# Four gate pairs of the second block computed as seven products, with fixed weight tiles and the memory's preparation moved

## The reference, cut to what matters

```python
branch_a = o_a @ w_branch_a[l]          # 512 -> 1024
branch_b = y_b @ w_branch_b[l]          # 512 -> 1024
merged = jax.nn.sigmoid(g_a) * branch_a + jax.nn.sigmoid(g_b) * branch_b
x = x + merged @ w_mix_out[l]
x = x + memory_cross_attention(rms_norm(x, norm_mem_q[l]), rms_norm(mem, norm_mem_kv[l]), ...)
```

## Time and profile before

| | us |
|---|---|
| median of 3 runs | 1548.76 (1548.67 to 1548.92) |
| profiled execution, its own time | 1548.38 |
| span of the trace | 1546.6 |
| PE busy | 1536.8 (99%) |
| DVE busy | 1055.0 (68%) |
| ACT busy | 754.5 (49%) |
| POOL busy | 69.1 (4%) |

### The profile page before, as it was taken

How to read it: one execution, slowest core, us unless ns; L and a number is a source line. 1 busy time by engine, 2 the same in 40 slices (tenths; PEclk the granted TensorE clock), 3 DMA queues, 4 the chain that set the end, 5 groups by cost and what they waited for, 6 DMA issues and landing times.

```text
span 1546.6 us, 22323 instructions
## 1 busy us (share of the span) xinstructions
PE 1536.8 (99%) x8348; PEld 1330.0 (86%) x8348; DVE 1055.0 (68%) x1755; ACT 754.5 (49%) x1307; POOL 69.1 (4%) x60
## 2 busy tenths in 40 slices
PE   9999999999999999999999999999999999999998
PEld 7888888888899899888888888888888899989987
DVE  6776887768789575447777545555555899948735
ACT  5446677744457445444544334344444445524514
POOL 0000000020000000210000010020002000000002
PEclk9999999999999999999999999999999999999999
DMA  5333222332323233324351242334123333322322
GB/s 195 122 109 97 88 78 93 103 129 90 127 84 110 96 96 108 97 82 131 118 141 62 71 137 87 118 118 156 55 82 109 110 103 110 124 96 82 110 89 75
DMA packets 56235, 161.88 MB, mean 105 GB/s; under 512 B 7232, under 2 KB 8640, under 8 KB 56000
## 3 DMA queue, kind: packets, MB, share of 16 engines
q1 hardware_dynamic: 55504, 159.41, 31.7%
q0 software_dynamic: 320, 0.52, 0.2%
q10 hardware_dynamic: 304, 0.52, 0.1%
HBM read 148.89 MB, written 2.10 MB: 98 GB/s over the span
## 4 chain that ended last, share of the span: by engine, by line
PE 96%; DVE 2%; ACT 1%; issue 1%; DMA 1%; SPq 0%; DVEq 0%; ACTq 0%
PE G L1490 66%; PE TP L1490 10%; PE SC L1490 9%; PE O L1490 5%; PE M L1490 5%; PE TP L1946 1%; PE TP L1892 0%; DMA T<-QK 0%; DVE WL L2623 0%; DMA GN<-in_gains 0%; PE TP L1995 0%; ACT L2030 0%; SPq L1465 0%; ACT WH L2033 0%; DVE T L2917 0%
## 5 line engine op out<-in xcount | busy, mean ns | idle before, releaser
L1490 PE MATMUL G<-XGh,WH 128*128 128x512 f32 x920 | 362.2, 394 | 0.0
L2623 DVE TENSOR_TENSOR WL<-RAW,WH 128x1024 fp32r<-128x1024 f32 (+2 forms) x269 | 282.7, 1055 | 116.5 <-ACT WH L2033 116.2
L1490 PE MATMUL G<-XGh,WL 128*128 128x512 f32 x920 | 358.4, 390 | 0.0
L1490 PE MATMUL G<-XGl,WH 128*128 128x512 f32 x920 | 358.3, 389 | 0.0
L2033 ACT ACTIVATE WH<-RAW 128x1024 fp32r<-128x1024 f32 (+2 forms) x275 | 240.0, 881 | 93.3 <-PE G L1490 60.8
L1490 PEld LDWEIGHTS G<-XGh,WL 128*128 128x128 f32 x920 | 172.7, 188 | 36.5
L1490 PEld LDWEIGHTS G<-XGh,WH 128*128 128x128 f32 x920 | 172.8, 188 | 36.1
L1490 PEld LDWEIGHTS G<-XGl,WH 128*128 128x128 f32 x920 | 172.9, 188 | 34.3 <-DVE XGl L2623 0.2
L1490 PE MATMUL G<-MGh,WH 128*128 128x512 f32 x372 | 145.0, 390 | 0.0
L1490 PE MATMUL G<-MGl,WH 128*128 128x512 f32 x372 | 144.8, 389 | 0.0
L1490 PE MATMUL G<-MGh,WL 128*128 128x512 f32 x372 | 144.7, 389 | 0.0
(11 more groups left out here) (443 smaller groups left out, 3268.8 us busy)
## 6 DMA issues: line engine op xcount, KB each, us to landing
RAW<-in_dn SPq DMA_DIRECT2D x30, 512.0 KB, 3.3
RAW<-in_fg SPq DMA_DIRECT2D x22, 512.0 KB, 4.2
RAW<-in_up SPq DMA_DIRECT2D x20, 512.0 KB, 3.4
RAW<-in_g SPq DMA_DIRECT2D x16, 512.0 KB, 3.4
RAW<-in_f SPq DMA_DIRECT2D x14, 512.0 KB, 3.7
X<-in_x SPq DMA_DIRECT2D x16, 256.0 KB, 4.3
RAW<-in_q SPq DMA_DIRECT2D x8, 512.0 KB, 3.3
RAW<-in_k SPq DMA_DIRECT2D x8, 512.0 KB, 3.4
```

The costliest lines, as they stand in the source:

```text
L1490: return e.matmul(dst, st, mv, start=start, stop=stop, skip_group_check=True)
L2623: return e.tensor_tensor(dst, src, hi.bitcast(F32), ALU.subtract)
```

## The change

- Gate pairs n = 4 to 7 are made by seven products (`seven_gates`; pairs `GATED` + n). Their units `sa n`, `sb n` are replaced by seven half-tile units each; `bb n` and `ba n` stay.
- `prepare_gates` makes the input's sums for them: per `kt`, `h` adds XGh and XGl back to fp32 for two tiles, then `s13`, `s2`, `s4`, `s_hi`, `s_lo`, in 13 ticks from ba 0's on. It writes `GATE_SUMS` (parts of QK, Vh, Vl).
- Half tile j of every such pair has slot j (0 to 6); from n = 4 on `bb n` has slot 7 and `ba n` slot 8. The rotation does not advance for them.
- The branch weights from bb 3 on land in `T` tiles of their own (6, then 0 for bb and 1 for ba from n = 4), not in `RAW`. SP waits for the last `s_lo` before bb 4's load.
- The closing part has sigmoids on ACT (`c11`, and `sigmoid` for the other parts); the gates land in one pair of tiles (RB, MSK) for all n from 3 on, so `c22`, `c11` and `c21` wait for `merge_b` of the pair before.
- `mem_load` is moved to behind the seven products of pair 7, its squares to the first three ticks of the mx units, the norm to tick 4, the splits to ticks 7 to 14; the low parts (`mem_lo`) are steps of their own, one tick after each high part.

```diff
+GATED, GATE_FIRST = MID + 20, 4
...
     for n in range(2, 8):
-        u += [("sa", n, 1024), ("sb", n, 1024), ("bb", n, 512), ("ba", n, 512)]
+        if n < GATE_FIRST:
+            u += [("sa", n, 1024), ("sb", n, 1024)]
+        else:
+            u += sevens(GATED - MID + n, GATED - MID + n + 1)
+        u += [("bb", n, 512), ("ba", n, 512)]
...
-            if name == "su":
+            if name == "su" and i[0] >= GATED - MID:
+                keys = (i[1],)
+            elif name in ("bb", "ba") and i >= GATE_FIRST:
+                keys = (7 if name == "bb" else 8,)
+            elif name == "su":
...
+    def prepare_gates(self, start):
+
+        for kt in range(4):
+            for n, kinds in enumerate((("h",), ("s13", "s2"), ("s4", "s_hi"), ("s_lo",))):
+                for kind in kinds:
+                    self.later(start + 3 * kt + n, kind, 2, kt)
+
+    def seven_gates(self, i):
+
+        f = GATED + i
+        for j in range(7):
+            self.tick()
+            if j == 0:
+                for n, kind in ((3, "one_out"), (3, "w_less"), (3, "v_less"), (4, "c22"), (5, "c11"), (6, "c12"), (6, "c21")):
+                    self.later(n, kind, f)
+                self.later(6, "sigmoid", f, 1)
+                self.later(7, "sigmoid", f, 0)
+            self.put("seventh", f, j, self.take("su", (f - MID, j)))
...
+        self.prepare_gates(0)
         for n in range(2):
             branch(n, 0)
             self.put("merge_b", n)
-        self.put("mem_load")
-        for k in range(8):
-            self.later(4 + k, "sq", "mem", k)
-            self.later(20 + k, "mem_split", k)
-        self.later(17, "norm", "mem")
         for n in range(2, 8):
-            gates(n)
+            if n < GATE_FIRST:
+                gates(n)
+            else:
+                self.seven_gates(n)
+            if n == 7:
+                self.put("mem_load")
             branch(n, 1)
             branch(n, 0)
             self.put("merge_b", n)
...
     def memory(self):
+        for k in range(8):
+            self.later(k // 3, "sq", "mem", k)
+            self.later(7 + k, "mem_split", k)
+            self.later(8 + k, "mem_lo", k)
+        self.later(4, "norm", "mem")
...
+                    if (name, i) == ("bb", 3):
+                        e.wait_ge(tb_done, TB["turn_b", 3, 2])
+                    elif name in ("bb", "ba") and i == GATE_FIRST:
+                        e.wait_ge(prep_dve, PREP_DVE["s_lo", 2, 3])
```

More of the change, by code:

```diff
@@ L251, in __init__ @@
         self.fetches, self.pairs = self.tail_loads(), [f for f in range(22) if ("st", f, 0) in self.item_of]
+        self.gated = [GATED + n for n in range(GATE_FIRST, 8)]
         self.middle = [MID + p for p in range(MID_FIRST, MID_FIRST + MID_PAIRS)]
@@ L1369, in _ @@
                         e.wait_ge(prep_dve, PREP_DVE["s_lo", 0, 3])
+                    elif name == "sums" and f == GATED + GATE_FIRST:
+                        e.wait_ge(tb_done, TB["turn_b", 3, 2])
+                    elif name == "sums" and f == GATED + GATE_FIRST + 1:
+                        e.wait_ge(mb_lo, MB["merge_b", 2])
                     if behind:
@@ L1618, in _, with left_of_gates @@
             left_of[6] = lambda kt: (Vh[:, 4 + kt, HALF_S:S], Vl[:, 4 + kt, HALF_S:S])
+            def left_of_gates(j, kt):
+                if j in (0, 1, 3, 5):
+                    s = (0, 1, 3, 5).index(j)
+                    h, l = GATE_SUMS[2 * (s // 2):2 * (s // 2) + 2]
+                    return h[:, s % 2, kt, :], l[:, s % 2, kt, :]
+                k, half = kt if j == 2 else 4 + kt, slice(HALF_S, S) if j == 6 else slice(0, HALF_S)
+                return XGh[:, k, half], XGl[:, k, half]
             for step in steps:
@@ L1677, in _ @@
                     mid = f >= MID
-                    first, second = (f == pair for pair in first_pairs[0 if mid else 1])
+                    gated = f >= GATED
+                    first, second = (f == pair for pair in first_pairs[2 if gated else 0 if mid else 1])
                     wh, wl = w_tile(q) if mid else item_tile(q)
@@ L1681, in _ @@
                     bank = bank[:, 0:HALF_S]
-                    if j == 0:
+                    if gated and (j == 0 and (first or second)):
+                        e.wait_ge(ob_lo, PVB["pv_b", 3])
+                    elif gated and first and j in (1, 3):
+                        e.wait_ge(wtb_lo, 2 * 16)
+                    elif gated and (j == 2 and (first or second)):
+                        e.wait_ge(sb_win, 12)
+                    elif j == 0:
                         if first and mid:
@@ L1720, in _ @@
                         at = slice(kt * P, (kt + 1) * P)
-                        hi, lo = left_of[j](kt)
-                        if first and j in (0, 2):
+                        hi, lo = left_of_gates(j, kt) if gated else left_of[j](kt)
+                        if gated and first and j == 0:
+                            e.wait_ge(prep_dve, PREP_DVE["s_lo", 2, kt])
+                        elif first and j in (0, 2) and not gated:
                             e.wait_ge(prep_dve, PREP_DVE["s_lo" if j == 0 else "a_lo", 0 if mid else 1, kt])
@@ L2114, in _ @@
                         e.wait_ge(d_mem, 16)
+                        if k == 0:
+                            e.wait_ge(w_lo, unit("su", (last_gated - MID, 6)))
                     else:
@@ L2406, in _ @@
                     e.wait_ge(unit_done, gemm_done(step))
-                    e.activation(sgb[n % 2][w], G[:, turn_of[step] % 2, :], ACT.Sigmoid).then_inc(g_moved, 1)
+                    e.activation(sgb[n][w], G[:, turn_of[step] % 2, :], ACT.Sigmoid).then_inc(g_moved, 1)
                 elif kind == "merge_b":
@@ L2526, in _ @@
                     e.wait_ge(*seven_done(f, 4))
[L2527 to L2528 removed]
+                    e.activation(made_in(f)[0][:, 0:HALF_S], SC[:, TURN7[f] % 2, 0:HALF_S],
+                                 ACT.Sigmoid if f >= GATED else ACT.Relu if f >= MID else ACT.Silu).then_inc(seven_act, 1)
+                elif kind == "sigmoid":
+                    f, w = arg
+                    table(ACT.Sigmoid)
+                    e.wait_ge(seven_dve, SEVEN_DVE["c12" if w else "c21", f])
+                    part = made_in(f)[1] if w else made_in(f)[0][:, HALF_S:S]
+                    e.activation(part, part, ACT.Sigmoid).then_inc(seven_act, 1)
                 elif kind == "silu":
@@ L3202, in _ @@
                     b, n = b_tiles(f), TURN7[f]
-                    first = f in (first_pairs[0][0], first_pairs[1][0])
-                    section = 0 if f >= MID else 1
+                    first = f in [pair[0] for pair in first_pairs]
+                    section = 2 if f >= GATED else 0 if f >= MID else 1
                     if not first and i in (1, 3):
@@ L3208, in _ @@
                         e.wait_ge(*lo_made)
+                    elif i == 1 and section == 2:
+                        e.wait_ge(mb_lo, MB["merge_b", 1])
                     elif i == 1:
@@ L3237, in _ @@
                     section, kt = arg
+                    if section == 2:
+                        if kt == 0:
+                            e.wait_ge(tb_done, TB["turn_b", 3, 2])
+                        else:
+                            e.wait_ge(prep_dve, PREP_DVE["s4", 2, kt - 1])
+                        for at, k in zip(halves_of(section, kt), (kt, 4 + kt)):
+                            t = e.tensor_tensor(at, XGh[:, k, :].bitcast(F32), XGl[:, k, :].bitcast(F32), ALU.add)
+                        t.then_inc(prep_dve, 1)
+                        continue
                     if kt == 0:
```

125 lines of the change are left out of this document (87 added, 38 removed).

## The result

The changed kernel took 1572.92 us (median of 4 runs, 1572.49 to 1573.96) against 1548.84 us (4 runs of the kernel before, 1548.67 to 1548.99): a ratio of 1.0156, 95% interval 1.0139 to 1.0174. It is slower by 24.1 us. I had predicted slower by 11.2, with 1563.5 us as the top of the range. The sign was right and the size was less than half.

A forecast was written before the change was run, and what follows sets the result against it. PE, busy 99%, was taken as the bound. Saved matmul time and waits, -3.24 + 0.4 + 1.6 + 3.6 + 3.0 + 2.7 + 3.1 = +11.2 us on 1548.76, gave 1560.0 us; range 1552.5 to 1563.5.

The forecast's parts named there:

- What bounds the kernel, and what can be won: Whole kernel: PE has nothing to spare, so saved matmul time, 3.24 us for four pairs, is the most to win.
- The waits of the preparation: Gate and branch stage: PE waits 0.4 us ahead of ba 2, 1.6 ahead of sa 3, 3.6 ahead of ba 3.
- no hole over 1.3 us: Sign: the DVE timeline from 883 to 935 us should have no hole over 1.3 us.
- Pairs 4 to 7: Product 4 waits for one_out: 3.0 us in pair 4, 1.36 each in pairs 5 and 6, 0 in pair 7.
- mx 0: First mx tile: its slot is freed only by ba 7's end, so PE waits 3.1 us.
- The low parts half a tile later run under mx 3 to mx 7 (27 us of matmuls): 0: Mx stage: the memory's low parts cost 0, or 1.1 us each if DVE were full there.
- The POOL additions I held for a risk at the norm's matmuls: Norm ahead of mx 2: squares' adds on POOL taken as 0, 3.1 us if each takes 1.48.
- the clock at 0: Longest waits: no clock loss in the sum; a possible 1.6 us each for two waits was left out.
- Worse: Rival, chance 0.10: POOL adds (3.1), pair 5's load (0.9) and a clock fall (1.6 to 3.2) on top, up to 1567.
- The preparation fits: Rival, chance 0.2: DVE and ACT have room before pair 4, the first three waits' 5.6 us go: 1554.0.
- the end is faster: Rival, chance 0.09: nothing waits at the branch multiplies, one_out or mx 0, -3.24 us: 1545.5.
- the load of pair 5: Pair 5's loads behind bb 4's on SP: up to 0.9 us late, taken as 0.

The follow-up runs named there:

- Run 7: Changed kernel with mx 0's tile in free slots, the memory's scaling half a tile earlier, and one_out, w_less and v_less earlier: 1555.79 us, ratio to before 1.0048.
- Run 8: Changed kernel with the next kt's sums of XGh and XGl put ahead of this kt's low parts, same number of operations: 1569.26 us.
- Run 4: Changed kernel with one_out of a gate pair two ticks earlier: 1569.8 us.
- Run 1: Changed kernel with the wide tile rotation advanced by one at mx 0, which so gets slots 4 and 5: 1566.98 us.
- run 3: Kernel before, with only the memory's squares, norm and splits moved as in the change, gates left as plain pairs: 1555.66 us, ratio 1.0043.
- Run 2: Changed kernel with the memory's scaling a step of its own, one tick ahead of the high part, three tiles in turn: 1566.62 us.
- run 5: Changed kernel with no half tiles prepared at sb 3, so its sigmoid comes first on ACT: 1574.37 us.
- run 6: Changed kernel with all eight sums of XGh and XGl in the gate section made by POOL instead of DVE: 1572.58 us.
- run 9's second kernel: Kernel of Run 7 with the sums reordered as in Run 8 and no half tiles prepared at sb 3: 1551.94 us, ratio to before 1.0023.

## Why the prediction was right and wrong

**What bounds the kernel, and what can be won: right.** PE was full, so the matmul time saved (3.24 us) was the most to win, and every wait is paid in full. Run 7 bears the second part out: with three repairs at once 17.1 us came back, 12.2 of which two of them had given alone.

**The waits of the preparation (0.4, 1.6, 3.6): right in place and size.** Run 8 shows that their cause is the order, not the load: the same operations, moved into the holes, took the first two away and a third of the last. My walk had the standing still in it ("two high parts on ACT between them, in which DVE stands still") and its three waits came out within 0.3 us. But "no hole over 1.3 us" between 883 and 935, one of my signs, was wrong: where ba's high part follows the preparation's on ACT, the hole is 1.74 us (at 902.26 and 920.05).

**Pairs 4 to 7: right in place; pair 4 too high (3.0, measured 2.20), pairs 5 and 6 too low (1.36, measured 1.60 and 1.95).** Together 5.75 against 5.72. Run 4 shows what stood behind: `v_less` in the same place as `one_out`, hidden until that was moved.

**mx 0: right (3.1, measured 3.22).** Run 1 took it away.

**The step that failed: "The low parts half a tile later run under mx 3 to mx 7 (27 us of matmuls): 0".** The memory's work in the mx stage cost 5.1 us of waits, and 6.8 us with what follows (run 3). I had asked whether DVE has room. It had: 14 of 20 us. What I had not done there, and had done in the gate stage, is to walk through both queues. Scaling on DVE, high part on ACT and low part on DVE make a round trip twice per unit, the unit's own high part stands behind it on ACT, and 7.37 us a unit is more than PE's 5.45. Run 2, which changes only the order (and gives the scaling a third tile), took 6.3 us off. The POOL additions I held for a risk at the norm's matmuls (3.1); they did not delay those, but held up one low part per unit by 1.1 us. What that hold-up costs alone was not tried; run 2 kept it and lost nearly all of the waits, so it was not the main part.

**The other step: the clock at 0.** The half clock took 6.0 us. I had the evidence and kept 1.6 us each for two waits for the rival "Worse" instead of the sum. Run 1 shows it for one wait: with the 3.2 us of wait went a stretch at 0.62 that cost 1.7 us more. The Trainium skill (TensorE: Matmul & The Clock Gate, Part 1) has an idle TensorE go to its half clock; the traces agree for every wait of 2.5 us or more here, and for the broken-up stretch ahead of `km`. With the clock and the memory's waits in the sum it would have been 11.2 + 5.1 + 6.0 = 22.3.

**Rivals.** "The preparation fits" and "the end is faster" are out; every wait that I walked through was there. "Worse" was the case that came, but neither of its first two terms (the adds at the norm, the load of pair 5) was part of it, and its top of 1567 was too low by 6. Its third term, the fall of the clock (1.6 to 3.2), was the one that came, twice as large.

**Left open.** The wait at 172 us, for a low part whose code the change does not touch: 0.4 in before, 1.0 in the changed kernel, and anything from 0.2 (run 8) to 1.0 (run 5) in the versions of it. Each was profiled once, so it may differ from execution to execution and not be the change's; that was not tried. And why the half clock behind a wait of 2.2 us comes or not: it did in runs 6 and 8 and not in the changed kernel. The traces show what goes with it, told below, and not the reason.

## What to carry to other kernels

When steps go back and forth between two engines that serve in order, spare room on average says nothing: walk through both queues in every stage that a step is moved to, count what stands behind the waiting instruction, and put other work into the hole rather than moving work to a third engine. A wait of a full TensorE must be priced with the half clock behind it, here 1.7 us on top of 3.2 and 2.6 on top of 3.8. And a change that wins 0.2% of matmul time can be eaten by one wait of 3 us, so the first question is not what it saves but what it puts into the queues.

## What the runs showed of the hardware

- **The half clock follows a wait.** A granted clock of 0.50 over 925 to 930 us behind a wait of 3.8 us, 0.62 over 4.5 us behind one of 3.2 (1.7 us lost), 0.66 over 5 us behind one of 2.5 (run 8). Behind single waits of 1.2 to 1.95 us (run 9's second kernel; pairs 5 and 6 of the changed kernel) the stretches stayed at 1.00. At 2.2 us both were seen. What goes with it is the stretch before: behind ba 3's wait the matmuls at half pace lasted 5.3 us in the changed kernel and 5.9 in run 1, and the wait at product 4 of pair 4 (2.20 and 1.81) brought none; in runs 2, 6 and 8 they lasted only 3.1 to 3.2 us, and that wait (2.35, 2.20 and 2.21) brought a second stretch of 3.4 to 3.6 us.
- **DVE waits for POOL.** In the mx stage an operation of DVE that starts during a POOL addition ends only after it: 1.51 us instead of 0.42 at 256 columns, 0.28 us behind the addition's end. In run 6 two of 512 columns took 1.77 and 1.44 us instead of 0.69 and ended 0.54 and 0.55 us behind the end of POOL's row; the one at 895.19, beside the first of that row's two additions, kept its 0.70. The kernel before has the same in its mx stage, where it is hardly seen, since the operation there is long and begins late in the addition (1.52 instead of 1.23 at 1024 columns):

```profile
1006.02 1.52 DVE L2623 TENSOR_TENSOR WL<-RAW,WH 128x1024 fp32r<-128x1024 f32 x1 [0.72 <-ACT WH L2033]
```

- **A stop has a small price of its own.** At full clock the first matmul behind a wait is 0.10 us dearer by starts: 0.22 instead of 0.12 at 256 columns (937.98 to 938.20 above), 0.33 instead of 0.23 at 512 (sa 3, 907.15 to 907.48). A whole product behind a wait takes 1.54 us from start to start (937.98 to 939.52) instead of 1.44; the chain's 1.70 is more than that.
